# Attention over 64-query chunks, unmasked, with two alternating output blocks, in a one-core transformer layer

## What is computed

```python
mod = silu(c) @ mod_w + mod_b                       # six vectors of 2048
h = rms_norm(x, g0) * (1.0 + sc_m) + sh_m
qkv = h @ w_qkv                                     # rotary on q and k, q scaled
s = einsum('bnqhgd,bnkhd->bnhgqk', qb, k_band)      # 64 queries x 128 keys per chunk
s = where(key_chunk >= 0, s, MASK_VALUE)            # chunk 0 has no chunk before it
p = softmax(concat([s, sink]))[..., :-1]
o = einsum('bnhgqk,bnkhd->bnqhgd', p, v_band)
x = x + gt_m * rms_norm(o @ w_o, g1)
h = rms_norm(x, g2) * (1.0 + sc_f) + sh_f
x = x + gt_f * rms_norm(swiglu(h, w_in, w_out), g3)
```

## Time and profile before

| | |
|---|---|
| Median of three runs | 1204.37 us (1202.93 to 1208.48) |
| The profiled execution: its time, its span | 1205.0 us, 1203.2 us |
| Granted TensorE clock, mean | 0.958 of full |
| Busy: PE, DVE, ACT, POOL | 1092.6, 694.7, 491.0, 43.2 us |
| Moved by DMA | 288.97 MB, 240 GB/s |
| Rotation of the first query column starts | 172.8 us |
| Last block of `w_o` (39) has been split | 426.3 us |

### The profile page before, as it was taken

The page is one execution under the profiler, slowest core; times in us unless marked ns, Lnnn a source line. Parts: engine busy times, 40 slices in busy tenths (PEclk is TensorE's granted clock), DMA queues, the critical chain, the costliest instruction groups (busy, mean ns, idle before and its releaser), DMA issues.

```text
span 1203.2 us, 13927 instructions
## 1 busy us (share of the span) xinstructions
PE 1092.6 (91%) x5032; PEld 875.4 (73%) x5032; DVE 694.7 (58%) x730; ACT 491.0 (41%) x609; POOL 43.2 (4%) x39
## 2 busy tenths in 40 slices
PE   5677887899779968999999999999999999999995
PEld 2455566677557756888888888888888888888884
DVE  0243289999987875567667544444444444444454
ACT  4132224675464444343343343334333443434443
POOL 0000010101000011000000000000000000000002
PEclk9878989889889999999999999999999999999998
DMA  9968868788879833678778554554545455555542
GB/s 381 422 262 371 318 241 312 263 293 313 305 259 373 321 115 133 230 278 298 262 284 299 209 202 174 202 182 177 206 177 191 160 206 177 207 179 205 183 166 70
DMA packets 50578, 288.97 MB, mean 240 GB/s; under 512 B 6384, under 2 KB 6384, under 8 KB 23792
## 3 DMA queue, kind: packets, MB, share of 16 engines
q1 hardware_dynamic: 49536, 286.29, 64.7%
q10 hardware_dynamic: 1008, 2.23, 0.5%
HBM read 286.40 MB, written 2.10 MB: 240 GB/s over the span
## 4 chain that ended last, share of the span: by engine, by line
PE 65%; DVE 14%; DMA 11%; ACT 4%; issue 4%; POOL 1%; SPq 0%; ACTq 0%; DVEq 0%
PE ps L1107 21%; PE ps L1108 20%; PE ps L1109 20%; DMA mraw<-in_mod_w 5%; DVE wlo L610 5%; DMA raw<-in_w_qkv 5%; DVE mraw L621 3%; ACT whi L334 3%; DMA mraw<-in_mod_h 1%; PE ps L1139 1%; PE ps L1129 1%; DVE hf L881 1%; ACT s L408 1%; DVE rtmp L679 1%; PE ps L1255 1%
## 5 line engine op out<-in xcount | busy, mean ns | idle before, releaser
L610 DVE TENSOR_TENSOR wlo<-raw,whi 128x2048 fp32r<-128x2048 f32 x172 | 394.2, 2293 | 369.9 <-ACT whi L334 369.7
L1107 PE MATMUL ps<-whi,hThi 128*128 128x512 f32 x1248 | 500.5, 401 | 46.6 <-DVE wlo L610 37.0
L334 ACT ACTIVATE whi<-raw 128x2048 fp32r<-128x2048 f32 x172 | 329.0, 1914 | 499.0 <-PE ps L1109 422.4
L1108 PE MATMUL ps<-wlo,hThi 128*128 128x512 f32 x1248 | 494.7, 396 | 0.0
L1109 PE MATMUL ps<-whi,hTlo 128*128 128x512 f32 x1248 | 494.6, 396 | 0.0
L1107 PEld LDWEIGHTS ps<-whi,hThi 128*128 128x128 f32 x1248 | 239.9, 192 | 105.2 <-issue 42.7
L1109 PEld LDWEIGHTS ps<-whi,hTlo 128*128 128x128 f32 x1248 | 239.5, 192 | 51.3
L1108 PEld LDWEIGHTS ps<-wlo,hThi 128*128 128x128 f32 x1248 | 240.3, 193 | 48.8
L621 DVE CUSTOM_DVE_ANT_0 mraw<-mraw,cb,modT 128x1024 f32<-128x1024 f32 x64 | 82.6, 1307 | 23.3 <-DMA mraw<-in_mod_w 23.3
L621 DVE CUSTOM_DVE_ANT_0 mraw<-mraw,cb,mbias 128x1024 f32<-128x1024 f32 x64 | 82.7, 1309 | 15.3 <-DMA mraw<-in_mod_w 15.1
L1107 PE MATMUL ps<-whi,oThi 128*128 128x512 f32 x128 | 52.4, 410 | 5.5 <-DVE wlo L610 3.5
(11 more groups left out here) (140 smaller groups left out, 545.5 us busy)
## 6 DMA issues: line engine op xcount, KB each, us to landing
raw<-in_w_in SPq DMA_DIRECT2D x88, 1024.0 KB, 4.8
mraw<-in_mod_w SPq DMA_DIRECT2D x128, 512.0 KB, 6.3
raw<-in_w_out SPq DMA_DIRECT2D x44, 1024.0 KB, 4.8
raw<-in_w_qkv SPq DMA_DIRECT2D x24, 1024.0 KB, 10.2
graw<-in_mod_h SPq DMA_DIRECT2D x20, 1024.0 KB, 16.5
raw<-in_w_o SPq DMA_DIRECT2D x16, 1024.0 KB, 8.3
mraw<-in_mod_h SPq DMA_DIRECT2D x12, 1024.0 KB, 13.3
x<-in_x ACTq DMA_DIRECT2D x2, 1024.0 KB, 7.4
```

Source lines behind the costliest of these rows:

```text
L334: A(whi[:, s % 2], raw[:, s], ACT.Copy).then_inc(hi_done, 1)
L610: V.tensor_tensor(wlo[:, s % 2], raw[:, s], whi[:, s % 2].bitcast(F32), ALU.subtract).then_inc(lo_done, 1)
L1107: mm(dst, hi, whi[:, s % 2, n], start=start, stop=False)
L1108: mm(dst, hi, wlo[:, s % 2, n], start=False, stop=False)
```

## The change

- Scores are made for each of the four 64-query chunks by itself. A score tile `ps[:, 2 + 2x + u]` holds four groups of 128 keys; its 128 rows are two heads times 64 queries. Nothing has to be masked: chunk 0 is multiplied with its 64 keys only.
- DVE takes the maxima straight from PSUM, ACT makes the exponentials from PSUM into `pS`. The mask, `s0`, `s1` and their two additions per round are gone.
- All keys are turned once, into `kT`; all values stay in `vr`, and the values of chunks 1 and 2 side by side are made by two small transfers from ACT's queue into `vS`. POOL's copies `kst` and `vst` are gone. There are 16 transposes of probabilities per turn where there were 24, four evictions where there were six, and 8 value products where there were 12.
- The work of a turn is written in another order. The first two columns of `w_o` alternate, block for block (`WO_ORDER`), in PSUM banks 6/7 and 0/1, and take blocks 24 to 31.
- SP's queue is written out as one list of pieces and blocks: 14 pieces per turn where there were 16, and four pieces ahead of each of the blocks 30 to 37.
- Loops over turns and columns are unrolled. Heads in `w_qkv`, `w_o` and `sinks` are permuted on the host.

```diff
-            for j in range(MPN):
-                if j == 2:
-                    load_first_w(11)
-                if j == 4:
-                    load_w(3, 0, block_src(w_qkv, 0, 1))
-                load_m(8, j)
...
-            def beside(i, w, cols, n, last=False):
...
-            with sp.Fori(1, 3) as i:
-                for s in range(4):
-                    q, r = (6 + i, 3) if s == 0 else (7 + i, s - 1)
-                    load_w(q, r, block_src(w_o, r, i if s == 0 else i + 1))
-                    for e in range(2):
-                        load_m(17 + i, 2 * s + e)
-            load_w(9, 3, block_src(w_o, 3, 3))
+            def load_mods(m, count):
+
+                for k in range(m, m + count):
+                    load_m(8 + k // MPN, k % MPN)
...
+            for i in range(3):
+                load_mods(8 + 14 * i, 4)
+                load_block(15 + 4 * i)
+                load_mods(12 + 14 * i, 4)
+                load_block(16 + 4 * i)
+                load_mods(16 + 14 * i, 3)
+                load_block(17 + 4 * i)
+                load_mods(19 + 14 * i, 3)
+                load_block(18 + 4 * i)
...
+            load_mods(60, 4)
+            load_block(30)
+            load_mods(64, 4)
+            load_block(31)
+            for g in range(32, 37):
+                load_mods(68 + 4 * (g - 32), 4)
+                load_block(g)
+            load_mods(88, 4)
+            load_block(37)
+            load_mods(92, 4)
+            for g in range(38, 41):
+                load_block(g)
...
+            for i in range(3):
+                if i:
+                    hi_of(12 + 4 * i)
+                    normalise(i - 1)
+                hi_of(13 + 4 * i)
+                if i:
+                    pT_out(i - 1)
+                hi_of(14 + 4 * i)
+                if i == 0:
+                    kT_out()
+                qT_out(i)
+                if i:
+                    oT_out(i - 1)
+                hi_of(15 + 4 * i)
+                probs(i, 0)
+                evac_q(i, 0)
+                probs(i, 1)
+                evac_q(i, 1)
...
+            hi_of(33)
+            square_y(1)
+            grow_evac(0, 2, 0)
+            hi_of(34)
+            grow_evac(1, 4, 0)
+            hi_of(35)
...
-                    V.tensor_tensor(s1[:, u, :, CHUNK:].rearrange("p (e m) k -> p e m k", e=2),
-                                    ps[:, 4 + 2 * u:6 + 2 * u, 0:6 * CHUNK].rearrange("p e (m k) -> p e m k", m=2),
-                                    mask[:].unsqueeze(1).unsqueeze(1).broadcast_to([P, 2, 2, 3 * CHUNK]),
-                                    ALU.add).then_inc(sc_read, 1)
...
+                if x == 0:
+                    s = ps[:, 2:4].rearrange("p u (y w k) -> p u y w k", y=2, w=2)
+                    V.tensor_reduce(mx[:, 0, :, 0:2], s[:, :, 0, :, 0:CHUNK], AX.X, ALU.max).then_inc(rmax, 1)
+                    V.tensor_reduce(mx[:, 0, :, 2:4], s[:, :, 1], AX.X, ALU.max).then_inc(rmax, 1)
+                else:
+                    V.tensor_reduce(mx[:, 1], ps[:, 4:6].rearrange("p u (t k) -> p u t k", k=P), AX.X,
+                                    ALU.max).then_inc(rmax, 1)
...
+            for i in range(3):
+                g, m = 12 + 4 * i, 8 + 14 * i
+                rope_q(i)
+                if i:
+                    denominator(i - 1, 1)
+                    lo_of(g)
+                mods(m, 4)
+                lo_of(g + 1)
+                mods(m + 4, 3)
+                lo_of(g + 2)
+                if i:
+                    oT_lo(i - 1)
+                mods(m + 7, 3)
+                max_and_sinks(i, 0)
+                max_and_sinks(i, 1)
+                lo_of(g + 3)
+                mods(m + 10, 2)
                 denominator(i, 0)
+                mods(m + 12, 2)
...
+            lo_of(31)
             oT_lo(3)
...
+            lo_of(32)
+            mods(68, 4)
+            lo_of(33)
+            mods(72, 4)
+            lo_of(34)
+            mods(76, 5)
+            lo_of(35)
+            mods(81, 5)
+            lo_of(36)
+            mods(86, 5)
...
             lo(9, 1)
+            mods(91, 5)
...
+            for i in range(3):
+                g = 12 + 4 * i
+                q_block(g)
+                if i:
+                    p_turn(i - 1)
+                q_block(g + 1)
+                if i == 0:
+                    k_turn()
+                q_turn(i)
+                if i:
+                    outputs(i - 1)
+                q_block(g + 2, (0,))
+                scores(i)
+                q_block(g + 2, (1,))
+                q_block(g + 3)
...
+WO_ORDER = [(0, 0), (0, 1), (1, 0), (1, 1), (0, 2), (1, 2), (0, 3), (1, 3)]
+WO_ORDER += [(n, k) for n in (2, 3) for k in range(4)]
```

More of the change, by code:

```diff
@@ L40 @@
 RMS_EPS = 1e-6
-MASKED = -1e30
 WP = 4
@@ L400, in _ @@
                     hi(3, 0)
[L402 to L411 removed]
+            act.wait_ge(half_evac, 4)
@@ L1437 @@
         "gT": np.ascontiguousarray(gains),
[L1438 to L1440 removed]
+        "w_qkv": blocks(w_qkv),
+        "w_o": blocks(w_o),
+        "sinks": np.ascontiguousarray(sinks),
         "w_in": blocks(inputs["ffn_w_in"]),
```

554 lines of the change are left out of this document (260 added, 294 removed).

## The result

The changed kernel takes **1256.91 us** (median; 1253.05 to 1258.09) against 1204.45 us before: a ratio of 1.0406, 95% interval 1.0364 to 1.0448. The forecast was 1243 us with a range of 1222 to 1262. The direction, the place and the mechanism of the main loss hold; the size was 14 us too small.

A forecast was written before the change was run, and what follows sets the result against it. DVE bounds the attention turns, PE the later `w_o` columns. Block 32 was put 17 us ahead, blocks 32 to 39 at 97.4 us against 42.3, so block 39 37.6 later; 1205.0 + 37.6 + 1.2 = 1243.8, forecast 1243 us, range 1222 to 1262.

The forecast's parts named there:

- The direction: Whole kernel: slower by 3.2%, with a chance of 0.87 for slower.
- the main loss: Blocks 32 to 39 of `w_o`: loads queue behind four pieces, so landings are paid in series; 97.4 us against 42.3.

The follow-up runs named there:

- e6: Against the changed kernel, modulation pieces 68 to 95 load only half of their columns, on stale data otherwise; 1245.86 us, ratio 1.0313.
- e9: Against the changed kernel, in each of three turns the fourth block's low split stands between the two halves' maxima instead of behind both; 1250.52 us.
- e7: Against the changed kernel, pieces spread 16 per turn, 24, then 16; loads follow them; ACT's and DVE's orders mended, second block's rounding moved; 1189.96 us, ratio 0.9857.

## What to carry to other kernels

Where one queue in order feeds two rings, a load's real lead is set by the item ahead of it whose slot frees last: if the last step ahead of the load's own user frees that slot, every round pays the landing in series. Here one round of lead gave all that more lead gave. An edit that measures zero can be worth 5 us after the next one, so keep it and measure it again when what covered it is gone. Work that is put off to a stretch bound by another engine is free there only as long as it fits beside that engine's work (16 pieces did, 28 didn't) and its loads do not stand ahead of those on which that engine waits.

## What I had not expected

- Halving the bytes of four transfers ahead of a block took only 1.9 of 8.9 us off its landing (e6), while the transfers rested half the time.
- Shortening a wait of 2.3 us on PE by 1.5 us gave twice that, 3.0 and 3.3 us per turn (e9): the clock stayed at its upper level.
- The last stretch can hold 16 pieces and 8 blocks in 43.3 us (e7), about as long as 9 pieces and 8 blocks took before (42.3), at 358 instead of 322 GB/s. The kernel before had room there.
